# Expert stage of a decoder layer: residual kept in PSUM, a ring of twelve units, experts in a loop, and another order for the last two

## The reference, cut to what matters

```python
h = h + merged @ w_out[l]
h = h + moe_ffn(rms_norm(h, norm_ffn_g[l]), w_router[l], b_router[l],
                w_up[l], b_up[l], w_down[l], b_down[l])
...
# moe_ffn: top 4 of 32 experts for each token, gates = softmax of the 4 logits
hdn = xb @ w_up[e] + b_up[e]                       # 1024 -> 2048
x_glu = jnp.minimum(hdn[:, :D_FF], SWIGLU_LIMIT)
x_lin = jnp.clip(hdn[:, D_FF:], -SWIGLU_LIMIT, SWIGLU_LIMIT)
act = x_glu * jax.nn.sigmoid(SWIGLU_ALPHA * x_glu) * (x_lin + 1.0)
return act @ w_down[e] + b_down[e]                 # 1024 -> 1024
...
h = rms_norm(h, norm_final_g)                      # rows of the 16 meta tokens dropped
```

## Time and profile before

| | us |
|---|---|
| median of 3 runs | 1204.7 (1204.47 to 1207.13) |
| the profiled execution's own time | 1205.39 |
| its span, first to last instruction | 1203.6 |
| PE busy | 1151.1 (96%) |
| DVE, ACT busy | 308.7 (26%), 187.2 (16%) |
| loads of the expert weights (SP's queue) | 192 of 2 MB |
| share of the chain that ended last | PE 63%, DMA 35% |

### The profile page before, as it was taken

The page is one execution under the profiler, slowest core; times in us unless marked ns, Lnnn a source line. Parts: engine busy times, 40 slices in busy tenths (PEclk is TensorE's granted clock), DMA queues, the critical chain, the costliest instruction groups (busy, mean ns, idle before and its releaser), DMA issues.

```text
span 1203.6 us, 12882 instructions
## 1 busy us (share of the span) xinstructions
PE 1151.1 (96%) x5632; PEld 533.9 (44%) x5632; DVE 308.7 (26%) x602; ACT 187.2 (16%) x378; POOL 0.2 (0%) x4
## 2 busy tenths in 40 slices
PE   8999999999999999999999999999999989999996
PEld 7767888845433333333333333333333333333332
DVE  4455620114222122212222121212221212121213
ACT  2257620012110100001110100000000000000002
POOL 0000000000000000000000000000000000000000
PEclk8999999999999999999999999999999999999999
DMA  9744434477999999999999999999999999999994
GB/s 372 275 168 172 150 116 169 173 279 279 406 429 427 427 428 427 426 428 427 427 429 427 427 427 429 428 426 428 427 429 428 427 427 427 428 426 429 427 427 174
DMA packets 36668, 442.46 MB, mean 368 GB/s; under 512 B 5312, under 2 KB 5824, under 8 KB 8320
## 3 DMA queue, kind: packets, MB, share of 16 engines
q1 hardware_dynamic: 33552, 438.09, 87.3%
q10 hardware_dynamic: 3056, 3.49, 0.8%
HBM read 440.52 MB, written 1.05 MB: 367 GB/s over the span
## 4 chain that ended last, share of the span: by engine, by line
PE 63%; DMA 35%; DVE 1%; ACT 1%; issue 0%; ACTq 0%; DVEq 0%
DMA ring<-in_w_exp_dram 23%; PE ps L867 19%; DMA work<-in_w_exp_dram 12%; PE ps L898 11%; PE ps L506 11%; PE ps L811 4%; PE ps L825 3%; PE ps L708 2%; PE ps L771 2%; PE ps L791 2%; PE ps L732 1%; PE ps L884 1%; PE ps L576 1%; PE ps L542 1%; PE ps L817 1%; DMA vec<-in_vec_dram 1%
## 5 line engine op out<-in xcount | busy, mean ns | idle before, releaser
L867 PE MATMUL ps<-ring,work 128*64 128x512 f32 x1504 | 339.6, 598 | 25.6 <-DMA ring<-in_w_exp_dram 25.2
L867 PEld LDWEIGHTS ps<-ring,work 128*64 128x64 f32 x1504 | 105.5, 137 | 251.8 <-issue 206.7
L1516 DVE TENSOR_TENSOR X<-ps,X 128x1024 f32<-128x1024 f32 x64 | 78.4, 1225 | 370.4 <-PE ps L825 370.4
L898 PE MATMUL ps<-ring,work 128*64 128x512 f32 x752 | 167.5, 595 | 0.0
L867 PE MATMUL ps<-work 128*64 128x512 f32 x544 | 123.1, 595 | 9.0 <-DMA work<-in_w_exp_dram 9.0
L506 PE MATMUL ps<-work,ring 128*128 128x256 f32 (+2 forms) x576 | 129.5, 384 | 0.0
L506 PEld LDWEIGHTS ps<-work,ring 128*128 128x128 f32 (+1 forms) x576 | 107.1, 188 | 19.1 <-issue 1.2
L1530 DVE TENSOR_SCALAR work<-ps 128x512 f32<-128x512 f32 x32 | 22.1, 692 | 338.1 <-PE ps L867 338.1
L1132 ACT ACTIVATE work<-work 128x512 f32<-128x512 f32 x32 | 20.2, 632 | 525.0 <-DVE work L1530 525.0
L898 PEld LDWEIGHTS ps<-ring,work 128*64 128x64 f32 x752 | 52.1, 137 | 98.0 <-issue 98.0
L867 PEld LDWEIGHTS ps<-work 128*64 128x64 f32 x544 | 37.9, 137 | 90.8 <-issue 73.0
(11 more groups left out here) (226 smaller groups left out, 622.1 us busy)
## 6 DMA issues: line engine op xcount, KB each, us to landing
ring<-in_w_exp_dram SPq DMA_DIRECT2D x141, 2048.0 KB, 46.2
work<-in_w_exp_dram SPq DMA_DIRECT2D x51, 2048.0 KB, 46.0
ring<-in_w_mix_dram SPq DMA_DIRECT2D x29, 1024.0 KB, 7.1
ring<-in_w_mix_dram SPq DMA_DIRECT2D x2, 576.0 KB, 18.4
ring<-in_w_mix_dram SPq DMA_DIRECT2D x4, 256.0 KB, 20.9
X<-in_x_dram ACTq DMA_DIRECT2D x2, 512.0 KB, 6.3
out_dram<-X SPq DMA_DIRECT2D x2, 512.0 KB, 2.6
ring<-in_w_mix_dram SPq DMA_DIRECT2D x1, 640.0 KB, 11.4
```

The lines of the kernel that those rows point to most:

```text
L867: ins = nc.tensor.matmul(ps[CAP * c:CAP * c + CAP, b, :], xeT[:, u // 2, k, CAP * (u % 2):CAP * (u % 2) + CAP], wu[:, k % SPAN, 512 * q:51 ...
L898: ins = nc.tensor.matmul(ps[CAP * c:CAP * c + CAP, 5, :], actT[:, j, CAP * g:CAP * g + CAP], wv[:, k, 512 * c:512 * c + 512], start=(f == ...
L1516: V.tensor_tensor(xi, ps[:, 6:8, :], xi, ALU.add).then_inc(scat_added, 1)
```

## The change

**Residual.** Banks 4 to 7 hold the sum from the start of the expert stage: `seed` writes `X` into them as a product with the identity (four products of 512 columns), and every scatter adds to them in place. `add_scattered` and its waits are gone. `X` moves into `work` and its place is reused by `hg`, `hl`, `sg` and `y`. The sum of the down biases becomes part of expert 0.

**Ring.** 12 units, two experts. `w_exp` is laid out in HBM as pairs of units: a partition's row is 32 KB, and each fetch still reads one unit, 16 KB of each row. The twelfth unit (1, 5) is fetched at `branch_read` 16, ahead of (1, 2).

**Experts.** 0 and 1 are written out, 2 to 29 are seven turns of a hardware loop of four, 30 and 31 are written out. Waits, DMA addresses and column numbers in the loop come from registers. Even experts have no `gather` and place both scatters behind the up products; odd ones have both scatters and `turn_route` among the up products and both halves of `gather` behind them. `xeT`, `gpickT` and the banks for transposes (3 and 2) are single.

**Last two.** The order is up 30, up 31, down 30, down 31; the fetches follow, and the last two units come in four pieces of 1 MB, with a wait for each.

**End.** ACT squares straight from PSUM; DVE multiplies by the final gain while that goes on; the scaling by token is split between DVE and ACT, and the output goes out in four transfers of 256 KB.

**Front.** `vec` is loaded on SP's queue behind two parts of `xT`; `x` there behind six blocks of mixer weights. `keep_clock_long` adds three products behind the sum of squares and one behind the spreading. `keep_clock(7, 4)` in the router is replaced by a `seed`.

```diff
@@ rings and fetches
-        RING = [ring_unit(j) for j in range(6)] + [spare_unit(0), spare_unit(1), ring_unit(6), ring_unit(7), spare_unit(2)]
+        RING = [ring_unit(j) for j in range(6)] + [spare_unit(0), spare_unit(1), ring_unit(6), ring_unit(7),
+                                                   spare_unit(2), spare_unit(3)]
+            spe.dma_start(vec[:, :], vec_in[:, :]).then_inc(vec_in_s, 16)
...
+                if n == 5:
+                    for k in range(TT):
+                        spe.dma_start(X[:, k, :], x_in[0, P * k:P * k + P, :]).then_inc(x_in_s, 16)
...
+            fetch(1, 0)
+            fetch(1, 1)
+            spe.wait_ge(branch_read, 16)
+            fetch(1, 5)
+            for c in (2, 3):
+                spe.wait_ge(weights_used, M0 - SLOTS + SPAN * (c + 5))
+                fetch(1, c)
             spe.wait_ge(xn2_ready, TT)
-            fetch(10)
-            for x in range(NR, E * UNITS_E):
-                spe.wait_ge(weights_used, M0 + SPAN * (x - NR + 1))
-                fetch(x)
+            fetch(1, 4)
+            with spe.Fori(0, (E - 4) // UNROLL) as it:
+                for u in range(UNROLL):
+                    for c in range(UNITS_E):
+                        r = UNITS_E * (u % 2) + c
+                        spe.wait_ge(weights_used, it * (UNROLL * PER_EXPERT) + (M0 + PER_EXPERT * u + SPAN * (c + 1)))
+                        spe.dma_start(RING[r], w_exp[it * UNROLL + (u + 2), c // 2, :, UNIT * (c % 2):UNIT * (c % 2) + UNIT])\
+                           .then_inc(unit_loaded[r], 16)
+            for n, c in [(E - 2, c) for c in range(4)] + [(E - 1, c) for c in range(4)] + [(E - 2, 4), (E - 2, 5)]:
+                spe.wait_ge(weights_used, M0 + PER_EXPERT * (n - 2) + SPAN * (c + 1))
+                fetch(n, c)
+            for t in range(4):
+                spe.wait_ge(weights_used, M0 + PER_EXPERT * (E - 3) + KT + SPAN * (t // 2 + 1))
+                spe.dma_start(RING[10 + t // 2][:, SLOT * (t % 2):SLOT * (t % 2) + SLOT],
+                              w_exp[E - 1, 2, :, SLOT * t:SLOT * t + SLOT]).then_inc(slot_loaded[8 + t], 16)
@@ TensorE
             ins.then_inc(xsum_done, 1)
+            keep_clock_long(2, xsq[:, 0, :], 3)
...
+            keep_clock_long(2, xsq[:, 0, :], 1)
...
+            def seed(i, c):
+                return nc.tensor.matmul(ps[:, 4 + 2 * i + c, :], ident, X[:, i, 512 * c:512 * c + 512], start=True, stop=True)
-            def scatter(u, i, it):
-                pe.wait_ge(scat_added, (it * UNROLL + u) * TT + (i + 1))
-                for c in range(2):
-                    ins = nc.tensor.matmul(ps[:, 6 + c, :], gpickT[CAP * c:CAP * c + CAP, (u + 1) % 2, i, :],
-                                           y[CAP * c:CAP * c + CAP, :], start=True, stop=True)
-                ins.then_inc(scat_done, 1)
+            def scatter(i, rows, turned):
+                for c in range(2):
+                    ins = nc.tensor.matmul(ps[:, 4 + 2 * i + c, :], turned[CAP * c:CAP * c + CAP, i, :],
+                                           rows[CAP * c:CAP * c + CAP, :], start=False, stop=True,
+                                           skip_group_check=True)
+            def even(n, unit_of):
+                up(0, unit_of, at_start, lambda k: None)
+                pe.wait_ge(y_ready, n + 1)
+                pe.wait_ge(gpickT_ready, n)
+                scatter(0, y, gpickT)
+                pe.wait_ge(route_ready, n + 1)
+                pe.wait_ge(hidden_read, n + 1)
+                up_bias(1)
+                scatter(1, y, gpickT)
+                pe.wait_ge(act_ready, n + 1)
+                turn_act().then_inc(actT_done, 1)
+                turn_route(2).then_inc(gpickT_done, 1)
+                pe.wait_ge(actT_ready, n + 1)
+                down(unit_of)
+            def odd(n, unit_of):
+                def between(k):                       # k-th of the eight steps of up
+                    if k == 1:
+                        pe.wait_ge(y_ready, n + 1)
+                        pe.wait_ge(gpickT_ready, n)
+                        scatter(0, y, gpickT)
+                    if k == 3:
+                        scatter(1, y, gpickT)
+                    if k == 5:
+                        pe.wait_ge(route_ready, n + 1)
+                        turn_route(2).then_inc(gpickT_done, 1)
+                up(1, unit_of, lambda k: None, between)
+                pe.wait_ge(pick_ready, n + 3)
+                gather(0).then_inc(gather_done, 1)
+                pe.wait_ge(gpickT_ready, n + 1)
+                gather(1).then_inc(gather_done, 1)
+                pe.wait_ge(hidden_read, n + 1)
+                up_bias(0)
+                pe.wait_ge(xeT_ready, n + 2)
+                pe.wait_ge(act_ready, n + 1)
+                turn_act().then_inc(actT_done, 1)
+                pe.wait_ge(actT_ready, n + 1)
+                down(unit_of)
...
+            gather(0).then_inc(gather_done, 1)
+            gather(1).then_inc(gather_done, 1)
+            seed(1, 1).then_inc(seeded, 1)
...
+            with pe.Fori(0, (E - 4) // UNROLL) as it:
+                for u in range(UNROLL):
+                    n = it * UNROLL + (u + 2)
+                    if u % 2 == 0:
+                        even(n, paired(it, u))
+                    else:
+                        odd(n, paired(it, u))
@@ ScalarE, ahead of expert 0
+            act.wait_ge(seeded, 1)
+            act.wait_ge(xn2_ready, TT)
+            act.wait_ge(hT_done, 2 * TT)
+            for c in range(2):
+                act.dma_start(y[CAP * c:CAP * c + E, :], b_down[0, :, 512 * c:512 * c + 512]).then_inc(bdn_in, 16)
+            for h in range(2):
+                act.wait_ge(gather_done, h + 1)
+                read_gather(h)
@@ VectorE
-            def add_scattered(n, i):
-                dve.wait_ge(scat_done, n * TT + (i + 1))
-                xi = X[:, i, :].rearrange("p (c n) -> p c n", c=2)
-                V.tensor_tensor(xi, ps[:, 6:8, :], xi, ALU.add).then_inc(scat_added, 1)
+            for i in (1, 0):
+                dve.wait_ge(last_scat, TT)
+                if i == 0:
+                    dve.wait_ge(f_sumsq, 1)
+                V.tensor_tensor(fin[:, i, :].rearrange("p (c n) -> p c n", c=2), ps[:, 4 + 2 * i:6 + 2 * i, :],
+                                gfin.rearrange("p (c n) -> p c n", c=2), ALU.mult).then_inc(gained, 1)
+            for i in range(TT):
+                dve.wait_ge(f_std, i + 1)
+                V.reciprocal(rsf[:, i:i + 1], rsf[:, i:i + 1]).then_inc(f_rs, 1)
+                dve.wait_ge(f_rs, i + 1)
+                dve.wait_ge(gained, TT)
+                V.tensor_scalar(fin[:, i, 0:512], fin[:, i, 0:512], rsf[:, i:i + 1], None, ALU.mult).then_inc(fin_dve, 1)
```

More of the change, by code:

```diff
@@ L134 @@
 M0 = len(LOADS)
+MIX_LANDINGS = [len(range(s, M0, SLOTS)) for s in range(SLOTS)]
 def load_width(kind, w):
@@ L796, in _ @@
             up_bias(0)
-            keep_clock(7, 4)
+            seed(0, 1)
             pe.wait_ge(mask_ready, 1)
@@ L903, in _, with last_start @@
             pe.wait_ge(flag_ready, 1)
             over = pe.value_load(flag_i[0:1, 0:1], min_val=0, max_val=1)
-            for it in range(GROUPS):
-                experts(it)
+            a, z = E - 2, E - 1
+            def last_start(k):
+                if k % 4 == 0:
+                    pe.wait_ge(xeT_ready, a + (k // 4 + 1))
+            up(0, alone(a, E // 2), last_start, lambda k: None)
+            pe.wait_ge(y_ready, a + 1)
+            pe.wait_ge(gpickT_ready, a)
+            scatter(0, y, gpickT)
@@ L1146, in _, with even @@
-            for it in range(GROUPS):
-                experts(it)
+            read_route(gpickT, 2).then_inc(y_ready, 1)
+            def even(n):
+                act.wait_ge(glu_ready, n + 1)
+                nc.scalar.activation(sg, hg, ACT.Sigmoid, scale=ALPHA).then_inc(sig_done, 1)
+                act.wait_ge(actT_done, n + 1)
+                read_act(actT, 3).then_inc(actT_ready, 1)
+                act.wait_ge(gpickT_done, n + 1)
+                read_route(gpickT, 2).then_inc(gpickT_ready, 1)
+                act.wait_ge(weights_used, n * PER_EXPERT + (M0 + PER_EXPERT))
+                nc.scalar.activation(y, ps[:, 3, :], ACT.Copy).then_inc(y_ready, 1)
@@ L1148, in _ @@
+            even(0)
+            odd(1)
+            with act.Fori(0, (E - 4) // UNROLL) as it:
+                for u in range(0, UNROLL, 2):
+                    even(it * UNROLL + (u + 2))
+                    odd(it * UNROLL + (u + 3))
             act.wait_ge(flag_ready, 1)
             over = act.value_load(flag_i[0:1, 0:1], min_val=0, max_val=1)
-            with act.If(over > 0):
-                with act.Fori(1, BLOCKS) as j:
-                    with act.Fori(0, GROUPS) as i:
-                        experts(j * GROUPS + i)
@@ L1166, in _ @@
+            for i in range(TT):
+                act.wait_ge(gained, TT)
+                act.wait_ge(f_rs, i + 1)
```

(14 more changed lines are left out.)

573 lines of the change are left out of this document (329 added, 244 removed).

## The result

The changed kernel takes 1192.38 us (median of 4 runs, 1190.5 to 1193.46); the kernel before, on the same chip, 1205.43 (4 runs, 1204.47 to 1207.13). The ratio is 0.9889, 95% interval 0.9874 to 0.9904: faster by 1.1%. The profiled execution took 1192.61 with a span of 1190.7, where 1193.5 and 1191.8 were forecast.

What follows compares the result with a forecast made beforehand. Weight transfers at about 427 GB/s were taken as the bound. Terms of -4.9 (twelfth unit), -3.5 (front), +1.75 (router) and -5.2 (end) sum to -11.9 us, giving 1193 us, range 1188 to 1206.

Steps and rivals of the forecast that it cites:

- three sums: Span as first fetch into a freed unit, stream to last landing, and tail: forecast changes -1.75, -4.9 and -5.2 us.
- What bounds the kernel: Expert stage: weights arriving at 427.5 GB/s set the pace, 29.4 us per expert; the end is stream start, stream and tail.
- PE per expert and its slack: Expert stage: even expert 25.7 us, odd 30.0, a pair 55.7 against 54.0 before, still under the weights' 29.4 per expert.
- The slack of 14: Expert stage: PE alone would reach the last down product at 1167.3, the weights allow about 1181.4; 14 us hide slower PE.
- The loop on PE: Looped experts: 0.6 us per turn plus 0.1 per expert for register waits, 7 us in all, hidden inside the slack.
- The rival at 1217: Loop turns fetch code at 5 us each, making PE the bound; chance 0.17, shared with a stream over 1% slower.
- The stream, the failed step: Expert weights: 180 units at 4.906 us plus the same 9.3 us of fill, unevenness and completion as before.
- The twelfth unit: Ring: one more unit is in before the stream begins, so the stream is 180 units: -4.9 us.
- Sums of the residual: Expert stage: DVE loses 64 passes of 1.225 us, which end no wait of PE: 0 us by itself.
- Front: Kernel start: earlier `vec` -1.5 us, added products keeping PE's clock up -2.0; together -3.5, between 0 and -4.
- Router, the second failed step: Before expert 0: third seed and two DMA issues of 0.34 us each delay ACT's copy: +1.75 us, between 0.9 and 2.6.
- End: From last landing to the end of the span: 12.2 us instead of 17.4, so -5.2, between -3.5 and -7.

Runs made afterwards that it cites:

- the kernel that copies first: Changed kernel with ACT's two copies of the gathered tokens ahead of its seed wait and two DMA issues for the down biases: 1187.8 us, ratio 0.9843.
- the one written out: Changed kernel with its loop of seven turns written out as straight code on all engines, nothing else: 1194.57 us, ratio 0.9905.
- the table late: ACT's early root, which loads its table, moved behind the branch, against the kernel that copies first: 1187.43 us.
- the kernel with eleven units: Changed kernel with the fetch of the twelfth unit (1, 5) held back until the first unit has been used: 1194.14 us.
- the base: The kernel that copies first: changed kernel with ACT's copies of the gathered tokens ahead of its two DMA issues, 1187.8 us.

## Why the prediction was right, and where it was right by chance

The forecast of 1193 against 1192.4 rests on three sums that were off by +3.7, -5.9 and +1.1 us, which cancel to -1.1.

- **What bounds the kernel.** Right. The stream at 427 to 430 GB/s sets the end; what moved the first fetch or the tail moved the time one for one (copy first -4.9 and -4.6, `vec` +1.1 and +1.1).
- **PE per expert and its slack.** Right: 25.73 and 29.9 us. The slack of 14 was against weights that would be there at 1181.4. In the kernel that copies first they are there at 1174.4 (7.0 earlier), and PE's own end moves from 1167.3 to 1163.6 (start 1.4 earlier, 15 pairs 0.15 shorter), so the same sum, redone with measured starts, gives 10.8. Measured: 10.0 to 10.6.
- **The loop on PE.** 7 us were taken, bounds 0 and 7.5 per turn; it is 0, with 55.55 us per pair with and without a turn. The rival at 1217 assumed that a turn makes PE fetch code that it has passed. It does not: from 450 to 1140 us no code packet comes. The Trainium skill (Runtime: NRT & Kernel Launch, "Instruction fetch mechanics") has a taken branch outside the fetched window stall for its fetch, a reason to write loops out. This case shows no such fetch in six turns, so it does not measure the stall; what it measures is that writing this loop out costs 4.7 us. A longer loop was not tried.
- **The stream, the failed step.** The step "180 units with the same 9.3" of fill and unevenness was wrong: 886.5 is 883.1 + 3.4. Written out, the stream gives 891.1, 892.3 and 891.8, that is 8.0, 9.2 and 8.7 over 883.1, near the 9.3 of before. I had named the code packets as a danger of the loop and not seen that the loop removes them: 27 packets, 0.42 MB. By bytes that is 1.0 us, by the queue's share (0.3% against 0.1% of 16 engines' span) 2.4. The rest is mostly the end of the stream, where the written-out kernels run at some half of the rate for about 5 us (1.9 to 2.0 us lost). It comes with the packets in all kernels, but how they would cause it is argued, not shown.
- **The twelfth unit.** -4.9 forecast; 3.4 to 3.7, since the transfers starve a little at 300 to 360 us.
- **Sums of the residual.** 0 forecast, and putting most of the work back on DVE (65 of 79 us) cost 0.1. The wait of PE for each sum was not put back. What the PSUM sum may bring through the tail was not tried by itself.
- **Front.** -3.5 forecast, -2.8 measured; its parts, tried one at a time, 1.1 for `vec` (forecast 1.5) and 1.5 to 2.0 for the clock (2.0).
- **Router, the second failed step.** "Issues two DMAs first (0.34 each)" was sized by SP's stores; ACT needed 1.93 us for the two in this kernel, 1.08 in the one written out. With the front's 2.8 used up in full, the part to the start of expert 0 cost 2.8, beyond its upper bound of 2.6. The clock behind the idle time, 1.9 more, was not in the forecast at all.
- **End.** 13.3 us behind the last landing, forecast 12.2, inside the bounds. Missing from the sum: two table loads of 1.28 on ACT (one delays the square; the root's stands beside it in DVE's passes). DVE's two gain passes, 2.35 us, begin 5.4 us behind the last landing, where some 4.8 was forecast. Nearly all of the gain comes from the order of the last two experts: without it the tail is 17.1 again, against 17.4 before, though 1.2 of that is the clock that falls behind PE's idle time there.

The kernel that copies first takes 1187.8 us and beats both (ratio to before 0.9843, 0.983 to 0.9857; with the table late 1187.4, not told apart from it). From before to there it is 18.3 us. What single undoings return is 4.7 (loop), 4.0 (order), 1.5 to 2.0 and 1.1 (front), and 3.4 to 3.7 (unit), together 14.7 to 15.5. What is left, about 3 us, is not assigned; up to 2.2 of it may be the layout.

## What to carry to other kernels

When transfers set the pace, add up the span as start of the stream, units times their time, and tail, and look for what else goes through the same queues: here writing a loop out put 26 code packets back among the weights and cost 4.7 us. Look at the rate in the last microseconds before the last landing: when it has dropped to half, some engines hold up the rest. An engine with slack hides what is added up to the slack and nothing beyond: 20.3 us on PE cost 9.7. The slack is PE's own end against the weights' (10.8 by the sum), not the total of its waits for weights (8 us). Before DMA issues are placed on a compute engine, ask what its next instruction is: here one copy behind two issues was the start of everything.

## What was not expected of the hardware

- The two DMA issues on ACT's queue ahead of expert 0 took 1.93 us in the changed kernel (one 0.33, the other 1.57), and between 1.08 and 2.62 in the twelve kernels of the experiments. ACT's other issues in the changed kernel take 0.32 to 0.45 each. In the changed kernel and the first one written out the DMA engines were still full with the last units of the ring as the issues began (426 and 344 GB/s from 282 to 283 us); the cause is not shown.
- After 2.66 us of idle PE the clock was granted at 0.50 for over 3 us, with PE busy all that time; after 2.74 us in the kernel with eleven units, and 1.81 in the one written out, it stayed at 1.00. The length of the idle time alone does not tell.
- A hardware loop of four experts had no visible turn on PE and fetched no code from its second turn on. Straight code of the same instructions slowed a saturated stream by 0.5 to 0.7% (891.1 to 892.3 against 886.5 us).
- With the loop and the copies first written out, the DMA engines move only about half of their rate (197 to 246 GB/s) in the last 5 us before the last landing; in the base they hold over 370 until 1 us before it.
